# Normalizing the residual after its reload, and the first root ahead of the second half's squares, in a two-block fp32 transformer kernel

## The reference, cut to what matters

```python
    return rms_norm(x, final_g)                      # end of the first block
...
    h = rms_norm_2(x, mix_pre_g[i]) * (1.0 + sc1) + sh1      # second block
    y = hybrid_mixer(h, w_in[i], ...)                # attention, causal convolution (31 taps), @ w_o
    x = x + g1 * rms_norm_2(y, mix_post_g[i])
    h = rms_norm_2(x, ffn_pre_g[i]) * (1.0 + sc2) + sh2
    y = swiglu_ffn(h, w_ffn_in[i], w_ffn_out[i])
    x = x + g2 * rms_norm_2(y, ffn_post_g[i])
```

## Time and profile before

| | |
|---|---|
| median of 3 runs | 2404.48 us (2403.85 to 2405.51) |
| the profiled execution | 2405.95 us, its span 2404.2 us |
| PE matmul busy | 2267.9 us, 94% of the span |
| DVE busy | 1475.4 us, 61% |
| POOL busy | 1404.4 us, 58% |
| ACT busy | 774.9 us, 32% |
| mean granted PE clock | 0.976 |

### The profile page before, as it was taken

How to read it: one execution, slowest core, us unless ns; L and a number is a source line. 1 busy time by engine, 2 the same in 40 slices (tenths; PEclk the granted TensorE clock), 3 DMA queues, 4 the chain that set the end, 5 groups by cost and what they waited for, 6 DMA issues and landing times. The chain is left out here.

```text
span 2404.2 us, 32299 instructions
## 1 busy us (share of the span) xinstructions
PE 2267.9 (94%) x11283; PEld 1887.9 (79%) x11283; DVE 1475.4 (61%) x2169; ACT 774.9 (32%) x1394; POOL 1404.4 (58%) x1359
## 2 busy tenths in 40 slices
PE   5999999999999999999979988899999999999995
PEld 3888889888888878877758867787888888888874
DVE  4835646587893999968899879747512222222236
ACT  4320113123121888833434267733210000000012
POOL 2555557565975888467898544376746433333360
PEclk8999999999999999999989989999999999999997
DMA  9345454424566665352243665442323211111121
GB/s 339 119 135 175 124 158 147 161 67 153 175 194 188 184 176 158 97 202 80 70 138 110 192 166 158 129 171 90 95 63 93 73 53 53 53 45 45 52 70 70
DMA packets 181039, 301.74 MB, mean 126 GB/s; under 512 B 34764, under 2 KB 73352, under 8 KB 179856
## 3 DMA queue, kind: packets, MB, share of 16 engines
q1 hardware_dynamic: 147120, 219.60, 32.1%
q10 hardware_dynamic: 33760, 80.07, 9.0%
HBM read 245.05 MB, written 54.56 MB: 125 GB/s over the span
## 5 line engine op out<-in xcount | busy, mean ns | idle before, releaser
L1215 PE MATMUL PS<-HXH,WH 128*128 128x512 f32 x1888 | 746.4, 395 | 33.1 <-ACT TM L1967 15.0
L1095 POOL TENSOR_SCALAR WH<-RAW 128x512 fp32r<-128x512 f32 x458 | 341.6, 746 | 704.4 <-PE PS L1217 553.6
L1216 PE MATMUL PS<-HXL,WH 128*128 128x512 f32 x1888 | 739.1, 391 | 0.0
L1217 PE MATMUL PS<-HXH,WL 128*128 128x512 f32 x1888 | 739.0, 391 | 0.0
L1098 POOL TENSOR_TENSOR WL<-RAW,WH 128x512 fp32r<-128x512 f32 x458 | 637.4, 1392 | 38.2
L1215 PEld LDWEIGHTS PS<-HXH,WH 128*128 128x128 f32 x1888 | 357.4, 189 | 115.9 <-POOL WL L1098 8.4
L1216 PEld LDWEIGHTS PS<-HXL,WH 128*128 128x128 f32 x1888 | 357.4, 189 | 74.9 <-issue 1.9
L1217 PEld LDWEIGHTS PS<-HXH,WL 128*128 128x128 f32 x1888 | 356.8, 189 | 75.5
L2622 DVE TENSOR_TENSOR TM<-PS,TM 128x512 f32<-128x512 f32 x44 | 29.3, 691 | 344.8 <-ACT TM L1998 339.1
L1998 ACT ACTIVATE TM<-PS 128x512 f32<-128x512 f32 x44 | 26.0, 598 | 534.5 <-PE PS L1217 533.4
L2635 DVE TENSOR_TENSOR Y<-PS,Y 128x2048 f32<-128x2048 f32 x40 | 91.7, 2292 | 117.5 <-PE PS L1217 115.4
(11 more groups left out here) (330 smaller groups left out, 4142.4 us busy)
## 6 DMA issues: line engine op xcount, KB each, us to landing
RAW<-in_ada_w SPq DMA_DIRECT2D x160, 256.0 KB, 2.9
RAW<-in_w_ffn_in SPq DMA_DIRECT2D x224, 128.0 KB, 2.1
RAW<-in_w_in_ab SPq DMA_DIRECT2D x88, 256.0 KB, 2.7
RAW<-in_w_in SPq DMA_DIRECT2D x56, 256.0 KB, 2.7
RAW<-in_w_ffn_out SPq DMA_DIRECT2D x56, 256.0 KB, 2.7
XX<-XR ACTq DMA_DIRECT2D x3, 4096.0 KB, 14.8
RAW<-in_w_in_c SPq DMA_DIRECT2D x40, 256.0 KB, 2.7
EARLY<-in_ada_w SPq DMA_DIRECT2D x32, 256.0 KB, 9.3
```

The source lines that it names most:

```text
L1095: g.tensor_scalar(WH[:, sw, 0:m], RAW[:, r, 0:m], 1.0, 0.0, ALU.mult, ALU.add).then_inc(gpsimd_done, 1)
L1215: mm(out, wh, xh, start=first, stop=False, **kw)
L1216: mm(out, wh, xl, start=False, stop=False, **kw)
L1217: return mm(out, wl, xh, start=False, stop=last, **kw)
```

## The change

Four edits. (1) At the start, `stat` h0 is written ahead of `sum` h1. (2) `xw` is taken out of the convolution and stands ahead of `wo` (1,h0), with a wait for the reload; `conv` -3 is written ahead of `flogz`; the spill now waits only for `XX` itself. (3) `R1`, which must now live until the output projection, gets 4096 bytes of its own. (4) For these, the scratch for dynamic DMA is set to 1024 bytes and all buffers start 15360 bytes lower.

```diff
@@ plan(), start
     ev("txc", "txc")
+    ev("stat", ("stat", 0, "h0"), n=0, part="h0")
     ev("sum", ("sum", 0, "h1"), n=0, part="h1")
-    ev("stat", ("stat", 0, "h0"), n=0, part="h0")
@@ plan(), convolution
         if (name, p) == ("cv", "h1"):
-            for x in x2:
-                ev("xw", ("xw", x), part=x)
+            ev("conv", ("conv", -3), i=-3)
             ev("flogz", "flogz")
-            ev("conv", ("conv", -3), i=-3)
             ev("spill", ("spill", 2, "h0"), n=2, part="h0")
@@ plan(), output projection
         w = weights("wo", g) if (g, p) != (0, "h0") else w_wo
+        if (g, p) == (1, "h0"):
+            for x in x2:
+                ev("xw", ("xw", x), part=x)
@@ buffers
-        slab = ctx.enter_context(nc.sbuf_tensor("slab", [P, 212000 // 4], F32))
+        slab = ctx.enter_context(nc.sbuf_tensor("slab", [P, 227328 // 4], F32))
-        BASE = 16512
+        BASE = 1152
+        EX = o[0]
-        R1 = {p: at(f"R1{p}", [HALF], F32, HREG + 77824 + 2048 * i) for i, p in enumerate(("h0", "h1"))}
+        R1 = {p: at(f"R1{p}", [HALF], F32, EX + 2048 * i) for i, p in enumerate(("h0", "h1"))}
@@ ACT, spill
-                        act.wait_ge(vector_done, upto("XW", n, part) if n == 2 else upto("XW", n))
+                        act.wait_ge(vector_done, upto("X", 2, part, 7) if n == 2 else upto("XW", n))
@@ DVE, xw
                     dve.wait_ge(vector_done, upto("r1", part))
+                    dve.wait_ge(x_loaded, upto("reload", 2))
@@ both builds
-    nc = bacc.Bacc("TRN2", target_bir_lowering=False, num_devices=1)
+    nc = bacc.Bacc("TRN2", target_bir_lowering=False, num_devices=1, dynamic_dma_scratch_size=1024)
```

More of the change, by code:

```diff
@@ L480, in program @@
         SM = small("SM", [64])
-        assert BASE + o[0] <= 229368, BASE + o[0]
+        EX = o[0]
+        assert BASE + EX + 4096 <= 229368, BASE + EX
         M = MREG
@@ L2941 @@
     arrays.update({f"in_{n}": x for n, x in shape_tables().items()})
-    counted = build(bacc.Bacc("TRN2", target_bir_lowering=False, num_devices=1), arrays, {})
-    nc = bacc.Bacc("TRN2", target_bir_lowering=False, num_devices=1)
+    counted = build(bacc.Bacc("TRN2", target_bir_lowering=False, num_devices=1, dynamic_dma_scratch_size=1024), arrays, {})
+    nc = bacc.Bacc("TRN2", target_bir_lowering=False, num_devices=1, dynamic_dma_scratch_size=1024)
     build(nc, arrays, counted)
```

## The result

The changed kernel takes 2409.41 us in the median (2407.51 to 2412.03, 11 runs), the kernel before, run beside it, 2403.85 us (2399.25 to 2405.51, 11 runs). The ratio is 1.0030, with a 95% interval of 1.0023 to 1.0038: **slower by 5.5 to 9 us**. The forecast was 2405.9, with 0.50 on no difference and 0.30 on slower. The measured time lies in the range, on the side that I had not put first.

What follows compares the result with a forecast made beforehand. PE, busy for 94% of the span, was taken as the bound. Start -1.6, convolution -8.6 and output projection +11.6 summed to +1.4 us on the median of 2404.48, giving 2405.9 us, range 2396 to 2412.5.

Steps and rivals of the forecast that it cites:

- no difference: Whole kernel: a measured time within 0.2% (4.8 us) of the kernel before, chance 0.50.
- Output projection: At `stat` 3 h0 PE waits 9.4 us for `xw` and loses 2.2 us to a slow clock: +11.6 us.
- The price from the stretch with the same POOL work: In `wo`: 1.35 us per multiplication, from two-tensor DVE operations at 1690.76 to 1696.12 that took 1.34 us each.
- full blocking: In `wo`: each multiplication waits for one POOL instruction; in the slower rival, 13.0 to 16.2 us wait, chance 0.19.
- Convolution: From `cg` h1 to `q2`: taking `xw` out and reordering `conv` -3 and `flogz` gains 8.6 us.
- The first restart: PE's restart behind its first sigmoid wait in `cg` h1 moves from 1244.07 to 1240.9, about 3.2 us earlier.
- The second: PE's restart behind its second sigmoid wait (fourth bank), at 1255.70 before, comes 9.5 us earlier.
- the half-speed stretch behind the wait I leave in: In the convolution: PE's slow clock behind the fourth-bank wait stays, since DVE's product still comes after PE has stopped.
- The start: Ahead of `ada` 1: PE's 5.03 us root wait goes, `apply` comes at 52 to 53 us; -1.6 us.
- `MOD` of `adac` 0 with them: At the start: this `MOD` runs behind the seven sums with the other `MOD` and coefficients, bringing `apply` to 52.4.
- The rival that ended slower by the cost of a multiplication: In `wo`: `xw` as slow as at its old place or at full blocking; net +5.0 to +8.2 us, chance 0.19.
- ACT and POOL did decide: Rival in the convolution: ACT and POOL set the pace, gain only 3.2 us, net +6.8, 2411.3 us; chance 0.10.

Runs made afterwards that it cites:

- e2: The changed kernel without the `xw` multiplications in either place, the residual keeping the first block's scale: 2399.21 us, ratio 0.9991 to the kernel before.
- e10: The changed kernel without the `xw` multiplications and with the root (`stat` h0) at its old place: 2395.54 us, ratio 0.9983 to the kernel before.
- e1: The kernel before with only `stat` h0 moved ahead of `sum` h1: 2402.56 us, ratio 1.0004 to the kernel before.
- e7: e4 with `adac` 0 moved ahead of `sum` h1: 2395.50 us, ratio 0.9976 to the kernel before.
- e6: The kernel before with only the memory edits (lower addresses, 1024-byte DMA scratch, own place for the root): 2400.14 us, ratio 0.9993 to the kernel before.
- e4: The changed kernel with `xw` of h1 back in the convolution behind `conv` -3, h0 still in `wo`: 2398.16 us, ratio 0.9986 to the kernel before.
- e11: e7 with `sum` h1 behind `apply` h0, its `stat` and `sum` c behind the first group: 2401.30 us, ratio 1.0003 to the kernel before.
- e12: e11 with `sum` c directly behind `sum` h1, ahead of the statistic of h1: 2397.71 us, ratio 0.9980 to the kernel before.
- e8: e7 with three fewer ACT and POOL taps in `conv` 0, moved to later convolution stages: 2397.11 us, ratio 0.9979 to the kernel before.

## Why the prediction was off, step by step

The mechanism was right in two of three terms, one of them mis-sized; the sum was +1.4 us, the stages that the change touches give +5.2, the medians +5.6, the ratio +7.2.

**Output projection: right.** 11.6 us predicted, 11.2 measured in the stage, 9.4 to 11.3 by the ratios (to e2 and to e10). The multiplications took 1.28 us in the mean for 1.35, the wait 9.28 us for 9.4, and the clock behind it was 0.50, as supposed; the slow stretch took 1.9 us (11.2 less 9.3) for 2.2. The price from the stretch with the same POOL work held, and the 1.78 us of the old place did not. That the wait came out within 0.2 us is in part luck: the multiplications took 1.1 us less in all than at 1.35, but they began 17.7 us ahead of the time at which PE stopped, where I had 18.5. One step of the reasoning was wrong and cost nothing in the sum: I took full blocking, as the Trainium skill (SBUF — State Buffer, section "Who interferes with whom") has it, for a rival with 13 us of wait or more, and 1.34 us against 0.75 plus a subtraction as a sign against it. The single rows above show each multiplication ending 0.53 to 0.56 us behind a POOL instruction, so the engines do take turns, and the trace agrees with that page. Since these 0.55 us are less than the 0.75 that a multiplication takes alone, and since every second split is a short one, taking turns comes to the 2.7 us for two multiplications that I had priced.

**Convolution: the restarts right, the sum mis-sized.** The first restart I had at 1240.9: 1243.20 less 2.2 is 1241.0. The second I had 9.5 us earlier, at 1246.2: 1248.52 less 2.2 is 1246.3. Here two errors cancelled: `flog` started 0.8 us later than I had said (1226.28 less 2.2, for 1223.3) and took 0.85 less up to the 24 taps (4.64 us for 5.49). ACT's and POOL's lead then let `q2` h1 start 8.0 us earlier (1273.33 less 2.2, for 1279.11), where I had 8.6. The step that failed is "the half-speed stretch behind the wait I leave in". I left it where it was. But whatever PE gains or loses between its restart and `q2` h1 does not count, since ACT and POOL decide when `q2` h1 starts: 56.1 to 56.3 us behind the start of the stage in all five profiles of this order (64.3 before), with waits of PE from 2.8 to 4.8 us there. The slow stretch that counts is the one behind this wait, where nothing absorbs it. Of the 8.0 us, 1.5 go in the first eight matmuls behind the wait and 0.5 later, and that leaves 6.0.

**The start: wrong.** I took -1.6 and it is 0 (58.9 and 58.9; e1 at 1.0004). I had followed the reciprocal to `apply` through DVE's queue alone. The step that failed is "`MOD` of `adac` 0 with them": I let both `MOD`s run at the end of the sums, but the second needs PE's `adac` 1, which needs the first one's bank, so a PE step of 3.57 us at the 1.2 GHz level came between them. e7 found a second holder behind the first, ACT's copy of `AROW`.

**The chances.** With 8.6 + 1.6 in place of 6.0 + 0, my sum was 4.2 us too low, and 0.4 too high in the output projection: that is the distance from +1.4 to +5.2, and between "no difference" and the measured 0.3%. The two large errors both stood on the side of the gain. The rival that ended slower by the cost of a multiplication was not what happened; ACT and POOL did decide at one place in the convolution; with the slow stretch behind it that took 2.6 us from my term, about half of the price that this rival had (8.6 less 3.2).

**What stays open.** By the ratios the convolution gives 2.2 us (e2) and 4.1 us (e10), where five profiles of the new order show 124.1 to 125.2 us against 130.3 and 130.4 in three of the old, so about 6. e10's interval holds 6 us, e2's ends at 4.3. Against e1, which has the same start, e2 gives 3.1 us, with an uncertainty of about 3 by the two intervals together. e6 speaks against the memory edits as the cause; the root is not excluded, since e1's interval reaches to +3.1 us, though no profile shows such a loss. Whether some 2 us are given back in executions that were not profiled was not settled.

## What to carry to other kernels

A queue that is emptied helps only if what stands behind the gap can start: look for who ends the next wait (here PE's gate logits), and move independent work into the gap rather than out of the stage. Half of the work left in its gap and half moved (e4) beat both all-or-nothing versions, because each place had room for about a half. When an edit removes a wait from the chain's first link, follow every engine that the next link passes through, banks and copies included, before you book a gain; and book a slow-clock stretch to the wait behind which no engine will absorb it, not to the one that is shortened.

## What the runs showed of the hardware

- An untouched stage varies between single executions: the 1156 us ahead of the convolution took 1153.8 to 1158.2 us in all kernels but e11 and e12, the start 57.2 and 58.6 with the same order and addresses (e6, e10), and `v2` with attention 200.4 to 205.2 us, once 207.5 (e8). In a single profile a gain under 5 us is to be read from its own stage, not from the span.
- DVE's two-tensor multiplication and POOL's splits lengthen each other, 0.75 to 1.28 us and 0.62 and 1.29 to 1.07 and 1.61 us, by taking turns: each multiplication beside full splits ends 0.53 to 0.56 us behind a POOL instruction. One pair of splits and the two multiplications beside it take 2.7 us, less than the 3.4 of their lone durations added up, since only 0.55 of a multiplication's 0.75 us fall behind the POOL instruction's end. So the price of the same multiplication follows from how long the POOL instructions beside it are: 1.78 us in the median beside additions, 1.1 and 1.78 by turns beside splits.
- A one-tensor `TENSOR_SCALAR` on 128x512 takes 0.49 us at its least and 1.02 in the mean beside the same splits: it takes turns with POOL as well, and ends 0.28 us behind a POOL instruction.
- Behind PE's idle times of 4.19 to 9.28 us in the convolution and in `wo` the mean granted clock of the 5 us from PE's restart was 0.50 to 0.70. For shorter ones it is not fixed: it was 1.00 behind 1.61 us (changed kernel) and 0.66 behind 2.00 and 2.78 us (e8), and the same wait of 2.30 us at 417 to 418 us, for DVE's `HXL`, was followed by 0.66 in the profile of before and by 1.00 in the changed kernel's:

```profile
417.20:422.20 5.00, 4.97 (x15) 3.97 (x16) 5.00 (x7) 4.97 (x13) 2.20 (x3) 0.66 0.33 108
```

```profile
418.00:423.00 5.00, 4.92 (x22) 4.11 (x23) 5.00 (x6) 4.97 (x13) 3.71 (x4) 1.00 0.36 108
```

  One wait of 3.33 us (e1, ahead of 1085.39) was also followed by 1.00, and one of 3.2 us at the same place before by 0.50. So a slow stretch behind a short wait comes in some executions and not in others, and it can be one source of the spread between them.
